# A two-block token mixer: part of the key preparation of the linear-attention stage moved from ScalarE and VectorE to GpSimd

## The reference, cut to what matters

```python
kk = heads(k * p['k_k']).astype(jnp.float32)
kk = kk / jnp.maximum(jnp.linalg.norm(kk, axis=-1, keepdims=True), 1e-12)
w_lat = jnp.tanh(wl)
for w0, w2, a0, a2 in (forward, backward):
    w = -jax.nn.softplus(-(w0 + w_lat @ w2).astype(jnp.float32)) - 0.5
    decay = jnp.exp(-jnp.exp(w))
    a = jax.nn.sigmoid((a0 + al @ a2).astype(jnp.float32))
    k_dir = k * (1.0 + (a - 1.0) * p['k_a'])
    dirs.append((heads(decay), heads(k_dir), heads(a)))
...
# the recurrence uses decay, k_dir, kk and b = kk * a
```

## Time and profile before

| | |
|---|---|
| median of 3 runs | 4349.22 us (4349.21 to 4351.21) |
| the profiled execution's own time | 4349.22 us |
| its span | 4347.4 us |
| TensorE busy | 3582.7 us (82%) |
| VectorE busy | 1978.5 us (46%) |
| ScalarE busy | 1235.1 us (28%) |
| GpSimd busy | 40.0 us (1%), 23 instructions |
| the four prepare stages together | about 140 us |

### The profile page before, as it was taken

One profiled execution on the slowest core, in us unless ns is written; L12 is line 12 of the kernel. 1 busy time (PEld: TensorE's weight loads), 2 busy tenths in 40 slices (PEclk: granted clock), 3 DMA queues, 4 the chain that ended last, 5 costly groups with the idle time before them and its releaser, 6 DMA issues. The chain is left out here.

```text
span 4347.4 us, 67478 instructions
## 1 busy us (share of the span) xinstructions
PE 3582.7 (82%) x28186; PEld 3126.3 (72%) x28186; DVE 1978.5 (46%) x2659; ACT 1235.1 (28%) x1810; POOL 40.0 (1%) x23
## 2 busy tenths in 40 slices
PE   4599978879797985699989946788996479998995
PEld 2488867759586763588877736777996479998874
DVE  2455276877775744444443354201221444444334
ACT  1313343333335732312222222111221232222222
POOL 0000000000000000000000000000000000000000
PEclk8799978879797997899999977899998789999997
DMA  4254310000005112111111121111212211111112
GB/s 168 85 153 152 119 38 3 21 20 3 1 3 120 41 35 82 44 48 43 48 34 47 43 81 49 39 42 37 61 54 83 79 48 44 48 44 34 48 41 90
DMA packets 225380, 247.09 MB, mean 57 GB/s; under 512 B 7471, under 2 KB 182910, under 8 KB 223118
## 3 DMA queue, kind: packets, MB, share of 16 engines
q1 hardware_dynamic: 225166, 243.99, 18.0%
HBM read 197.31 MB, written 46.65 MB: 56 GB/s over the span
## 5 line engine op out<-in xcount | busy, mean ns | idle before, releaser
L520 PE MATMUL psum<-h_hi,w_hi 128*128 128x342 f32 (+1 forms) x1824 | 590.5, 324 | 100.4 <-DVE w_lo L553 100.4
L520 PE MATMUL psum<-h_hi,w_lo 128*128 128x342 f32 (+1 forms) x1824 | 588.2, 322 | 0.0
L520 PE MATMUL psum<-h_lo,w_hi 128*128 128x342 f32 (+1 forms) x1824 | 587.4, 322 | 0.0
L520 PEld LDWEIGHTS psum<-h_hi,w_hi 128*128 128x128 f32 x1824 | 346.6, 190 | 103.6 <-DVE w_lo L553 103.6
L520 PEld LDWEIGHTS psum<-h_hi,w_lo 128*128 128x128 f32 x1824 | 346.7, 190 | 0.0
L520 PEld LDWEIGHTS psum<-h_lo,w_hi 128*128 128x128 f32 x1824 | 346.7, 190 | 0.0
L1921 ACT ACTIVATE xs<-psum 128x1024 f32<-128x1024 f32 (+1 forms) x88 | 90.6, 1030 | 785.2 <-PE psum L520 785.2
L520 PE MATMUL psum<-h_hi_ffn,w_hi 128*128 128x512 f32 x704 | 278.8, 396 | 30.3 <-DVE w_lo L553 30.3
L553 DVE TENSOR_TENSOR w_lo<-w_raw,w_hi 128x1024 fp32r<-128x1024 f32 (+1 forms) x152 | 177.1, 1165 | 259.9 <-ACT w_hi L532 259.9
L520 PE MATMUL psum<-h_hi_ffn,w_lo 128*128 128x512 f32 x704 | 280.8, 399 | 0.0
L520 PE MATMUL psum<-h_lo_ffn,w_hi 128*128 128x512 f32 x704 | 279.0, 396 | 0.0
(11 more groups left out here) (331 smaller groups left out, 6860.3 us busy)
## 6 DMA issues: line engine op xcount, KB each, us to landing
w_raw<-in_w_up SPq DMA_DIRECT2D x88, 512.0 KB, 3.8
w_raw<-in_w_in SPq DMA_DIRECT2D x58, 512.0 KB, 5.4
w_raw<-in_w_down SPq DMA_DIRECT2D x88, 256.0 KB, 2.6
mod_w<-in_w_mod SPq DMA_DIRECT2D x16, 1024.0 KB, 6.1
x<-x_scratch SPq DMA_DIRECT2D x3, 4096.0 KB, 12.6
rw_scratch<-conv_out SPq DMA_DIRECT2D x14, 640.0 KB, 7.4
x_scratch<-x SPq DMA_DIRECT2D x2, 4176.0 KB, 13.4
mod_w<-in_w_mod SPq DMA_DIRECT2D x4, 2048.0 KB, 10.0
```

The lines of the kernel that those rows point to most:

```text
L520: last = nc.tensor.matmul(out, w[s][:, kk, :], x[:, kk, c0:c0 + cn], start=(kk == 0 and q == 0), stop=(kk == kt - 1 and q == 2))
```

## The change

The factor is no longer made by ScalarE: VectorE makes it, after the normed `kk`. Its two buffers are now `k.tmp` and a new `k.tmp2`. The filling of `keep` and all four products of the factor with the key (`key_first` and the two last ones) go to GpSimd, which gets a list of its own in this stage. GpSimd waits for `factor` before each first product and for `b_made` before each second one, since that product overwrites what L1050 reads; VectorE's running sum waits for `marked`, GpSimd's signal that `keep` is filled. A drain is added between the two scalar_tensor_tensor of each direction.

```diff
-    k.factors = [k.at(f"factor{d}", [ALL], o[0] + 4 * ALL * d) for d in range(2)]
+    k.tmp2 = k.at("tmp2", [ALL], o[0])
...
-    factor = sem(f"prep{p}_factor")
+    factor, b_made = (sem(f"prep{p}_{n}") for n in ("factor", "b_made"))
+    factors = (k.tmp, k.tmp2)
+    marked = sem(f"prep{p}_marked")
...
-                act.wait_ge(gates, 2 * d + 2)
-                nc.scalar.activation(k.factors[d][:, :], k.pd[d][4][:, :], ACT.Identity, scale=prm("k_a"),
-                                     bias=k.omk[:, p:p + 1]).then_inc(factor, 1)
...
-            nc.vector.memset(k.keep[:, :], 1.0)
-            dve.drain()
-            nc.vector.memset(k.keep[:, 0:ALL:CH], 0.0)
-            dve.drain()
-
             def cumulate(d):
                 dve.wait_ge(gates, 2 * d + 1)
+                dve.wait_ge(marked, 1)
...
-            def key_first(d):
-                dve.wait_ge(factor, d + 1)
-                nc.vector.tensor_tensor(k.pd[d][3][0:64, :], k.factors[d][0:64, :], k.kx[0:64, :], ALU.mult)
-
             cumulate(0)
...
-            key_first(0)
             cumulate(1)
             dve.wait_ge(norms, 1)
             nc.vector.tensor_tensor(k.kk[:, :], k.kk[:, :], ps[0][:, 0:ALL], ALU.mult)
-            key_first(1)
             dve.drain()
             for d in range(2):
                 first, second = k.pd[d][3], k.pd[d][4]
+                dve.wait_ge(gates, 2 * d + 2)
+                nc.vector.tensor_scalar(factors[d][:, :], second[:, :], prm("k_a"), k.omk[:, p:p + 1],
+                                        ALU.mult, ALU.add).then_inc(factor, 1)
                 nc.vector.scalar_tensor_tensor(out=first[64:P, :], in0=second[64:P, :], scalar=-1.0, in1=k.kk[64:P, :],
-                                               op0=ALU.mult, op1=ALU.mult)
+                                               op0=ALU.mult, op1=ALU.mult).then_inc(b_made, 1)
+                dve.drain()
                 nc.vector.scalar_tensor_tensor(out=second[0:64, :], in0=second[0:64, :], scalar=-1.0, in1=k.kk[0:64, :],
                                                op0=ALU.mult, op1=ALU.mult)
-            dve.drain()
+
+        @block.gpsimd
+        def _(pool):
+            nc.gpsimd.memset(k.keep[:, :], 1.0)
+            pool.drain()
+            nc.gpsimd.memset(k.keep[:, 0:ALL:CH], 0.0).then_inc(marked, 1)
             for d in range(2):
-                nc.vector.tensor_tensor(k.pd[d][4][64:P, :], k.factors[d][64:P, :], k.kx[64:P, :], ALU.mult)
+                first, second = k.pd[d][3], k.pd[d][4]
+                pool.wait_ge(factor, d + 1)
+                nc.gpsimd.tensor_tensor(first[0:64, :], factors[d][0:64, :], k.kx[0:64, :], ALU.mult)
+                pool.wait_ge(b_made, d + 1)
+                nc.gpsimd.tensor_tensor(second[64:P, :], factors[d][64:P, :], k.kx[64:P, :], ALU.mult)
```

## The result

The changed kernel takes 4390.82 us (median of 4 runs, 4388.60 to 4391.94) against 4349.22 us of the kernel before: a ratio of 1.0095, 95% interval 1.0078 to 1.0112, +41.6 us. The forecast was 32 us slower (4381), with a range from 4357 to 4390, so the direction was right and the time lies 0.8 us above the range. The profiled execution took 4385.28 us, 36.1 us more than that of the kernel before. It is the fastest of the five on record and is not among the four: with it the median would be 4389.96, just inside the range.

What follows compares the result with a forecast made beforehand. VectorE's 10.42 us tail was taken to end each prepare stage; with both engines end to end, 0.07 + 1.90 + 5.96 + 11.56 - 7 x 0.15 = 18.4, +8.0 a pair, so 4349.2 + 32 = 4381 us, range 4357 to 4390.

Steps and rivals of the forecast that it cites:

- What bounds the stage: Prepare stages: VectorE's 10.42 us tail after the kk multiply sets the end; work removed before it is worth nothing.
- The price of the operations: Tail of each prepare stage: VectorE factor 0.95 us, scalar_tensor_tensor of 64x1280 1.49, GpSimd product 2.89.
- Laid end to end, 18.4 us: Tail: VectorE and GpSimd exclude each other, 18.4 us against 10.42, +8.0 a pair, +32 in four; chance 0.55.
- VectorE's second factor waits too: Tail, direction 1: the factor cannot run beside a GpSimd product; 32 us in all if it waits, 28 if not.
- The meeting after GpSimd: Prepare stage's end: GpSimd's meeting could differ from VectorE's 0.76 us by a few tenths, about 1 us in four.
- Side-by-side halves: Tail: GpSimd's products on the two partition halves overlap but still shut VectorE out; +3.2 us a pair, 4362; chance 0.20.
- rival 2: Tail: VectorE and GpSimd on different halves, or at this shape at all, do not collide; +2.2 a pair, 4358; chance 0.09.
- rival 3: Tail: partition half decides collisions, one mechanism for both engines; +0.4 us a pair, 4351, or 4346; chance 0.08.
- the handover: Tail: seven turns between engines may each add 0.15 us instead of hiding it; 2.1 us more a pair, +40 in all.
- theory A: Around the four longer stages: TensorE stays at its lower granted clock longer, about 2.4 us each; changed kernel again +38 to +43.

Runs made afterwards that it cites:

- E7: Kernel before with only the filling of keep (two memsets) moved to GpSimd, plus the wait for `marked`: 4352.43 us, -2.8 (0.9998).
- E4: Changed kernel with the normed kk also written to PSUM, read there by the four scalar_tensor_tensor: 4374.39 us, +22.3 against the kernel before (1.0052).
- E10: The kernel before, unchanged, measured as if it were a change: 4354.25 against 4352.49 us, +1.8 (0.9999).
- filler kernel: Kernel before with 8.1 us of useless VectorE work behind each of the four prepare-stage tails, nothing on GpSimd: 4386.91 us (+34.9) and 4388.55 us (+36.5).
- E3: Kernel before with 32 us of useless VectorE work once, behind the tail of pair 3's prepare stage: 4385.49 us, +33.4 (1.0075).
- E5: Changed kernel with the four products given back to VectorE, GpSimd only filling keep: 4368.14 us against 4355.21 of the kernel before, +12.9 (1.0029).
- E6: Changed kernel with the two factors given back to ScalarE in their own buffers, products left on GpSimd: 4372.09 us, +16.9 against the kernel before (1.0036).
- E8: Kernel before reordered without GpSimd: separate buffer for a, products before the kk multiply, later sums and square root: 4342.44 against 4355.21 us, -12.8 (0.9970).
- E2: Kernel before with 8.1 us of useless VectorE work behind each of the four tails, first measurement: 4386.91 us, +34.9 (1.0080).
- E1: The changed kernel measured again, no edit: 4387.19 us against 4352.06 of the kernel before, +35.1 (1.0082).
- E12: Kernel before with 8.1 us of useless VectorE work behind each of the four tails, second measurement: 4388.55 us, +36.5 (1.0086).
- E11: The changed kernel measured again, no edit, beside the filler kernel: 4389.16 us against 4352.07 of the kernel before, +37.1 (1.0092).

## Why the prediction was right or wrong

**What bounds the stage: right.** Up to the kk multiply nothing moved (22.57 us into the stage, as before), though VectorE's first tensor_scalar was held up by the memset (1.80 in place of 0.89) and its wait before the second running sum grew from 2.88 to 4.27 us. The work taken off VectorE and ScalarE there was worth nothing. E7 shows the memset's part by itself.

**The price of the operations: right.** Factor 0.95 (forecast 0.95), scalar_tensor_tensor 1.49, product 2.90 in E4 (forecast 2.89).

**Laid end to end, 18.4 us: right.** 18.40 us in the profile of the changed kernel. That the two engines shut each other out is shown by E4, which takes away the second SBUF input and with it the waits. That VectorE's second factor waits too, which had no row before, is shown at 1178.63 (3.49 us). The turns hide 0.14 to 0.27 us, and nothing is added at them. The meeting after GpSimd takes 0.82 us (1190.46 to 1191.28) against 0.76 after VectorE.

**The rivals.** Side-by-side halves fell: in E4 the second product waits for the first. No collision at half width (rival 2) fell too: a product and a scalar_tensor_tensor of 64 partitions wait for each other. The collision is not decided by halves either (rival 3): the first product, on partitions 0 to 63, waits for the scalar_tensor_tensor on 64 to 127 and takes 4.19 us.

**The step that failed** is the last of the sum, "4349.2 + 32 = 4381": the +32 was right (the stages measure 32.2), but I set it on a base as if the rest of the kernel repeated exactly, which puts every change outside the four stages at nothing without a reason, and gave the range above it room only for the handover (to 4390). The rest of the span, outside the four stages, was 4216.3 us in the profile that I started from, the lowest of fourteen; in the others it lay from 4218.2 to 4226.1 us with kernels of every kind, the unchanged one at 4221.6 (E10). The three runs shown agreed to 2 us and hid this; the kernel before later ran from 4346.4 to 4362.8. Of the 9.4 us above 32.2, the two profiles place 3.9 outside the stages (4216.3 against 4220.2), and the other 5.5 is the distance of the profiled execution (4385.28) from the median of the four (4390.82). Some of the 9.4 is therefore scatter: the further measurements leave 2.9, 5.2 and 4.9. Taken together, the 67 executions of the kernel before (those of E10 among them) have a mean of 4353.2 us, 4.0 above my base, and the 18 of the changed one 4389.4, 36.2 more and so again 4.0 above the 32.2.

**What stays open.** Those three leftovers, and the 2.7 and 4.3 us of the filler kernel with equal stages (10 executions, 35.5 us above the mean of the kernel before), all lie above zero, while E3 leaves 1.2 and E10, no change at all, shows 1.8. The other kernels, less their stages, leave +3.8 (E4), -1.4 (E5), +1.4 (E6), -2.8 (E7) and -0.7 (E8). These go largely with the group: the one of E5 to E8, whose kernel before had the highest median (4355.21), has three of its four below zero. A real cost of some 3 or 4 us that comes with longer stages, and not with GpSimd, would fit; chance with these group offsets is not ruled out, since each interval is 8 us or more wide. Of theory A, that TensorE stays at its lower clock longer around the longer stages, the traces show no sign. Worked out from each profile's granted clock and span, TensorE's time at the lower level (1.2 GHz) outside the four stages was about 775 and 796 us in the two profiles of the kernel before, and 787, 797, 780 and 774 in the four of the changed one; and of these six the one with the least of it (774) has the longest rest (4223.8 us). What the clock costs in one stage or another no run separates. Against GpSimd as the cause stand E2 beside E1 and E12 beside E11, 0.3 and 0.6 us apart.

## What to carry to other kernels

Work moved to an idle engine is worth only what it takes off the chain that ends the stage, and it does not run in parallel with what it left if the instructions of both engines take two inputs from SBUF: count the two as one queue, unless one of VectorE's operands can lie in PSUM (E4). Look first for waits in the timeline that a reordering can fill; here a separate buffer for a, the products moved into VectorE's waits, and a later sum on TensorE with its square root on ScalarE, all changed at once, gave 12.8 us where a second engine cost 32. And when a sum is made against one execution, the scatter of the rest of the kernel belongs in the range, however closely three runs agree.

## What the runs showed of the hardware

- A memset on GpSimd and a tensor_scalar on VectorE hold each other up in both directions: 1.80 us in place of 0.89 for VectorE's, and 0.63 in place of 0.13 for GpSimd's memset of 20 columns. In pair 0, where they did not meet (VectorE's first instruction starts at 555.68), that memset took 0.13:

```profile
549.74 0.13 POOL L1051 MEMSET keep<- 128x20 f32 x1
```

- An instruction as small as 128x20 waits until a GpSimd product that began before it has ended (1152.37 to 1154.45, 2.08 us in place of 0.18; the product ends at 1154.41, E6).
- GpSimd's products on partitions 0 to 63 and 64 to 127 run one after the other, 2.90 us each (E4). That is what the 2.34 us of 128x1024 gives for 1280 elements: half the partitions save nothing.
